# Prompt attention of a hybrid encoder step: p in two rounded parts as stationary operand, v's parts and ones moving, and the streams' first k loaded earlier

## What is computed

```python
def fox_block(qi, cq, qpos, k, v, ck):
    logits = jnp.einsum('bqhd,bkhd->bhqk', qi, k, preferred_element_type=jnp.float32) * scale
    logits = logits + cq[..., :, None] - ck[..., None, :]
    mask = jnp.arange(k.shape[1])[None, :] <= qpos[:, None]
    logits = jnp.where(mask, logits, -jnp.inf)
    p = jax.nn.softmax(logits, axis=-1).astype(v.dtype)
    return jnp.einsum('bhqk,bkhd->bqhd', p, v)
```

## Time and profile before

| | us |
|---|---|
| median of 3 runs | 4081.55 (4078.66 to 4081.91) |
| the profiled execution's own time | 4079.91 |
| its span | 4078.4 |
| the stretch with the prompt's attention | 785 to 1785 of the span |
| TensorE busy in it | 945.66 of 1000 |
| VectorE and ScalarE busy in it | 495.96 and 370.97 |

### The profile page before, as it was taken

How to read it: one execution, slowest core, us unless ns; L and a number is a source line. 1 busy time by engine, 2 the same in 40 slices (tenths; PEclk the granted TensorE clock), 3 DMA queues, 4 the chain that set the end, 5 groups by cost and what they waited for, 6 DMA issues and landing times. The chain is left out here.

```text
span 4078.4 us, 55142 instructions
## 1 busy us (share of the span) xinstructions
PE 3826.5 (94%) x20813; PEld 3215.9 (79%) x20813; DVE 1643.1 (40%) x3406; ACT 1237.3 (30%) x2275; POOL 379.5 (9%) x367
## 2 busy tenths in 40 slices
PE   7999999699999999999979979999999999799996
PEld 7999999577777777776744449999999999677875
DVE  4000476555545455444323324444444444332122
ACT  4111222233333343332113333333333333222122
POOL 3000000211111111121100000000000000021122
PEclk9999999799999999999889989999999999899998
DMA  4221221411122111134233221111111111441221
GB/s 146 68 67 63 66 67 64 88 37 46 35 45 57 43 38 36 40 116 146 102 107 105 93 74 45 45 42 45 51 49 42 45 45 35 135 131 49 85 85 56
DMA packets 319131, 278.63 MB, mean 68 GB/s; under 512 B 121314, under 2 KB 269394, under 8 KB 318887
## 3 DMA queue, kind: packets, MB, share of 16 engines
q1 hardware_dynamic: 298703, 247.21, 20.5%
q0 software_dynamic: 5040, 18.09, 1.3%
q10 hardware_dynamic: 15228, 11.10, 1.0%
HBM read 190.70 MB, written 85.65 MB: 68 GB/s over the span
## 5 line engine op out<-in xcount | busy, mean ns | idle before, releaser
L2337 PE MATMUL bank<-hn_hi,up_w_parts 128*128 128x436 f32 (+1 forms) x3520 | 981.5, 360 | 10.1 <-DVE up_w_parts L2412 10.1
L2337 PEld LDWEIGHTS bank<-hn_hi,up_w_parts 128*128 128x128 f32 x3520 | 661.9, 188 | 42.0 <-issue 10.2
L2337 PE MATMUL bank<-hn_lo,up_w_parts 128*128 128x436 f32 (+1 forms) x1760 | 632.7, 359 | 0.0
L2337 PEld LDWEIGHTS bank<-hn_lo,up_w_parts 128*128 128x128 f32 x1760 | 331.3, 188 | 19.2
L332 PE MATMUL bank<-proj_wh,proj_xh 128*128 128x256 f32 (+1 forms) x1088 | 309.6, 285 | 0.0
L332 PE MATMUL bank<-proj_wh,proj_xl 128*128 128x256 f32 (+1 forms) x1088 | 306.7, 282 | 0.0
L332 PE MATMUL bank<-proj_wl,proj_xh 128*128 128x256 f32 (+1 forms) x1088 | 306.7, 282 | 0.0
L2383 ACT COPY up_raw<-bank 128x436 f32<-128x436 f32 (+1 forms) x220 | 110.5, 502 | 641.9 <-PE bank L2337 611.9
L1432 PE MATMUL bank<-heads_p_pT,heads_p_v 128*65 128x512 f32 (+3 forms) x640 | 288.2, 532 | 10.3 <-issue 10.1
L2586 PE MATMUL bank<-down_w_hi,down_g_hi 128*128 (+1 forms) x748 | 237.7, 400 | 50.1 <-DVE down_g_lo L2681 42.7
L2681 DVE TENSOR_TENSOR down_g_lo<-down_g_raw,down_g_hi 128x256 fp32r<-128x256 f32 (+1 forms) x198 | 110.1, 556 | 391.3 <-ACT down_g_hi L2646 391.3
(11 more groups left out here) (404 smaller groups left out, 6634.9 us busy)
## 6 DMA issues: line engine op xcount, KB each, us to landing
up_w<-in_w_up_dram SPq DMA_DIRECT2D x44, 512.0 KB, 4.7
down_g_raw<-scratch_g SPq DMA_DIRECT2D x88, 256.0 KB, 2.6
scratch_g<-up_acc SPq DMA_DIRECT2D x88, 218.0 KB, 2.0
heads_s_k<-in_cache_fox_k_dram SPq DMA_DIRECT2D x8, 2048.0 KB, 12.6
heads_s_v<-in_cache_fox_v_dram SPq DMA_DIRECT2D x8, 2048.0 KB, 8.1
heads_d_qkvT<-scratch_gch SPq DMA_DIRECT2D x17, 768.0 KB
down_y<-in_w_down_dram SPq DMA_DIRECT2D x22, 512.0 KB, 3.7
scratch_gch<-proj_work SPq DMA_DIRECT2D x48, 218.0 KB, 1.9
```

The lines of the kernel that those rows point to most:

```text
L2337: mm = pe.matmul(bank[:, pair(n) + e, 0:width], w_parts[:, a, part, e, k, :], x[:, k, cols], start=(k == 0 and m == 0), stop=(k == KD - 1 ...
```

## The change

p is now kept in two float32r parts. ScalarE takes exp twice for each block, once rounded into `p_hi` and once in float32 into `p`; VectorE subtracts them into `p_lo`. v is split once per head into `v_parts`, 130 columns a block: v's high part (64), two columns of ones, v's low part (64). The product is turned round: for each 128 queries of a block, `p_hi` (128 x 128) is stationary and all 130 columns of `v_parts` move, then `p_lo` is stationary and the first 66 columns move. The fourth tile of 128 queries has no room for 130 columns in the bank, so its `p_hi` goes in two products, of 66 and of 64 columns. The result stands as queries by columns, so the four transposes of each group go; ScalarE copies 128 x 456 (`raw`), and VectorE adds the parts and divides. v has one buffer for loading in place of two; f, its sums and the rows of c lie in places of p. k and q of the two parities are tensors of their own, and the streams' k of streams 0 and 1 is laid in those of even heads and loaded in the prompt's last head. The planned times are set anew.

```diff
-    PERIOD = 72.0
+    PERIOD = 66.0
...
-    SPEED = 0.62
+    SPEED = 0.57
...
-            return 2.65e-3 * sum(self.width(G, b) for b in range(self.blocks(G))) + 0.95e-3 * first + 1.6 + \
+            return 2.0e-3 * sum(self.width(G, b) for b in range(self.blocks(G))) + 0.95e-3 * first + 1.2 + \
...
-            pe.wait_ge(s["p_ready"], u + 1)
-            pe.matmul(self.bank[0:self.FD + 1, self.out, BANK - wide:BANK], self.v[:, h % 2, b, :],
-                      self.pT[:, u % 3, BANK - wide:BANK], start=(b == 0), stop=(b == last)).then_inc(s["pv_mm"], 1)
+            pe.wait_ge(s["lo_ready"], u + 1)
+            for i in range(4 - wide // P, 4):
+                cols, out = slice(i * P, (i + 1) * P), self.bank[:, self.out, i * VW:i * VW + (VW if i < 3 else VS)]
+                hi, lo = self.p_hi[:, u % 3, cols], self.p_lo[:, u % 2, cols]
+                last = b == 4 * g + 3
+                pe.matmul(out, hi, v[:, 0:VW if i < 3 else VS], start=(b == 0 and i == 0), stop=False)
+                if i == 3:
+                    pe.matmul(out[:, 0:FD], hi, v[:, VS:VW], start=False, stop=False)
+                mm = pe.matmul(out[:, 0:VS], lo, v[:, 0:VS], start=False, stop=last)
+            mm.then_inc(s["pv_mm"], 1)
...
-            nc.scalar.activation(self.pT[:, u % 3, BANK - wide:BANK], self.bank[:, self.keys[u % 2], BANK - wide:BANK],
-                                 ACT.Exp).then_inc(s["p_ready"], 1)
+            nc.scalar.activation(self.p_hi[:, u % 3, cols], logits, ACT.Exp)
+            after(act, s["lo_ready"], u - 1)
+            nc.scalar.activation(self.p[:, u % 2, cols], logits, ACT.Exp).then_inc(s["p_ready"], 1)
...
-            if G >= 1:
-                act.wait_ge(s["row_mm"], self.use["o", G - 1] + 1)
-            nc.scalar.copy(self.oT[:], self.bank[0:self.FD + 1, self.out, :]).then_inc(s["oT_ready"], 1)
+            after(act, s["o_ready"], 2 * G)
+            nc.scalar.copy(self.raw[:], self.bank[:, self.out, 0:self.RAW]).then_inc(s["raw_ready"], 1)
...
+            nc.scalar.copy(self.v_parts[:, h % 2, :, 0:FD], self.v[:]).then_inc(s["v_hi"], 1)
...
+            dve.wait_ge(s["p_ready"], u + 1)
+            after(dve, s["pv_mm"], u - 1)
+            nc.vector.tensor_tensor(self.p_lo[:, u % 2, cols], self.p[:, u % 2, cols],
+                                    self.p_hi[:, u % 3, cols].bitcast(F32), ALU.subtract).then_inc(s["lo_ready"], 1)
...
+            nc.vector.tensor_tensor(self.v_parts[:, h % 2, :, self.VS:self.VW], self.v[:],
+                                    self.v_parts[:, h % 2, :, 0:FD].bitcast(F32), ALU.subtract).then_inc(s["v_lo"], 1)
...
+            nc.vector.reciprocal(self.inv[:, a, 0:3], three[:, :, FD]).then_inc(s["inv_ready"], 1)
+            nc.vector.reciprocal(self.inv[:, a, 3:4], fourth[:, FD:FD + 1]).then_inc(s["inv_ready"], 1)
+            tt(three[:, :, 0:FD], three[:, :, 0:FD], three[:, :, VS:VW], ALU.add).then_inc(s["inv_ready"], 1)
...
-        yield self.prompt.end - 30.0
+        last_head = (self.prompt.FH - 1) * self.prompt.NG
+        yield self.prompt.group_at[last_head + 2]
+        sp.wait_ge(self.prompt.s["pv_mm"], self.prompt.first_key[last_head + 1])
         load_k(0)
+        load_k(1)
```

More of the change, by code:

```diff
@@ L1340, in sums @@
             pe.wait_ge(s["f_step"], NB)
-            pe.matmul(out, c["tri"][:], self.f[:].rearrange("p n h -> p (n h)"), start=True, stop=False)
-            pe.matmul(out, c["ones"][:], self.before[:].rearrange("p n h -> p (n h)"), start=False, stop=True) \
+            pe.matmul(out, c["tri"][:], self.f.rearrange("p n h -> p (n h)"), start=True, stop=False)
+            pe.matmul(out, c["ones"][:], self.before.rearrange("p n h -> p (n h)"), start=False, stop=True) \
                 .then_inc(s["row_mm"], 1)
@@ L1415, in keys_tensor @@
             after(pe, s["p_ready"], u - 1)
[L1416 to L1417 removed]
+            pe.matmul(out, self.k_hi[a][:, keys], self.q_both[a][:, cols], start=True, stop=False)
+            mm = pe.matmul(out, self.k_lo[a][:, keys], self.q_hi[a][:, cols], start=False, stop=b < 4 * g)
             if b >= 4 * g:
@@ L1470, in keys_scalar @@
             u, wide = self.first_key[G] + b, self.width(G, b)
+            logits, cols = self.bank[:, self.keys[u % 2], BANK - wide:BANK], slice(BANK - wide, BANK)
             yield at + 1.6
@@ L1736, in tensor @@
                 pe.wait_ge(self.prompt.s["row_free"], len(self.prompt.uses))
+                pe.wait_ge(self.prompt.s["raw_ready"], self.prompt.groups)
             turn_k(0, n)
@@ L1876, in vector @@
         yield self.begin + 0.3
-        dve.wait_ge(self.prompt.s["row_free"], len(self.prompt.uses))
+        dve.wait_ge(self.prompt.s["o_ready"], 2 * self.prompt.groups)
         nc.vector.memset(self.q_heads[:], 0.0).then_inc(s["new_ready"], 1)
```

168 lines of the change are left out of this document (94 added, 74 removed).

## The result

The changed kernel takes **4174.33 us** (median of 4 runs, 4168.61 to 4183.89), the kernel before 4080.2 (4 runs, 4078.66 to 4081.91): a ratio of 1.0234 (1.0218 to 1.025). It is slower by 94 us where 46 were forecast. The direction was right and the time lies in the range, near its upper end, but the added time is twice the predicted one.

The account below looks back on a forecast made before the run. TensorE was taken to bound the prompt's stretch; +46 (product with v) - 15 (transposes) + 15 (waits) + 0 (rest) on 4079.9 gave 4126 us, 1.1% slower. Range 4090 to 4180 with 0.70, 4083 to 4185 for 8 in 10.

Parts of the forecast that it names:

- The bound: In the prompt's attention, 785 to 1785 us, TensorE sets the pace: busy 946 us of 1000, VectorE 496, ScalarE 371.
- The load of p's parts: Product with v on TensorE: 2,496 products at 0.112 us each, 280 us against 234, so 46 us longer.
- Rival A: Product with v: loads hide or are quicker than read; 3955 us, or 4048 at 0.081 us a product; chance 7%.
- The transposes: TensorE's 128 transposes of finished groups go, 9 us, with the 6.6 us waited before them: -15 us.
- The waits: TensorE's waits, mostly on VectorE, grow with its busy share: +15 us, between -20 and +60.
- VectorE and ScalarE: In the prompt's stretch ScalarE goes from 371 to about 549 us, VectorE from 496 to about 722; both stay beside TensorE.
- Rival C: VectorE or ScalarE takes over at L1513's wait on the second exp: 0.3 us a block, 96 us, 4207 us; chance 7%.
- The clock: TensorE in the prompt's stretch was expected to stay at full clock, with no time added for it in the sum.
- Rival D: Narrow products lower TensorE's clock: a tenth of the prompt's 1,045 us at 1.2 GHz adds about 50 us, 4176; chance 4%.
- The planned times: Order on the engines: the product stands 4.0 planned units behind its logits as before; the new times were costed at nothing.
- The early k: The streams' first two k loads move into the prompt's last head: nothing gained, bounds -5 and +5 us.
- Rival B: Added time falls where TensorE stood idle, 40 of 54 us closing: 4086 us; 10% for within 0.2%, 2% for faster.

Follow-up runs that it names:

- the best version here: The changed kernel with v's parts stationary, p's parts moving, and the high products ahead of the wait for p's low part: 4069.35 us, ratio 0.9971.

## Why the prediction was right in direction and wrong in size

- **The bound was read rightly.** TensorE sets the pace in the prompt's stretch, before and after.
- **The load of p's parts: right.** Forecast were loads 0.11 us apart and 2,496 x 0.112 = 280 us; the timeline shows 0.112, and the account 274, 0.110 each. The product of before holds 239 us, not 234. The term is +35 for a forecast of +46. Rival A, that the loads hide, is out. The Trainium skill, "TensorE: Matmul & The Clock Gate", section "Back-to-back issue gap", has 0.081 us for such pairs, and the timeline's 0.112 speaks against it here. The choice was made by the row with 4 moving columns, the right one.
- **What a narrow product does to the one behind it: left out.** The first wide product behind one of 66 columns ends 0.07 to 0.08 us later than behind a wide one (0.31 against 0.24): +13 us in all. The prediction said that a load hides only behind a product that is longer, and applied this to the new products but not to their successor.
- **The transposes: right.** -16 for -15.
- **The waits: the sum was nearly right, by luck; the working wasn't.** Of idle time, 6.6 us went with the transposes, and +15 was forecast on top; TensorE's idle time went from 55 to 66.5, so +18 on top. But the forecast grew all waits on VectorE with its busy share. What grew is one wait, that on p_lo before L1436, by 27 us, while those of `Delta`, of the maxima and of the turning of q and k shrank by 11. The text had called this chain covered, "since the product stands in TensorE's list as far behind its logits as before (4.0 planned units), with more work between". With an exp and a subtraction more in the chain, the same distance did not cover it. The mark that was set, over 60 us of idle time that ends with L1563 or L1513, is not reached: 26.6 and 3.6.
- **VectorE and ScalarE: as forecast, a little less.** 698 and 510 us of the 1,100 for 722 and 549. Rival C has fallen as a sum: its place, the wait of L1513 for the second exp, holds 81 us, 0.25 us for each of 320 blocks where it had 0.3, but little of it reaches TensorE. The row maxima queued behind end 3.6 us of L1375's idle time, and p's low part itself 26.6 of L1436's, where the rival had 96.
- **The clock: the step that failed.** The sum took the prompt's stretch at full clock, and so the clock at nothing. Full clock was named as a mark, and is what is not there. Another mark, TensorE busy for 25 to 40 us longer, shows the same: it is busy for 86 us longer (1031.5 for 945.9), and for 31 when the clock's 55 are taken off. Rival D had the mechanism (narrow moving parts in runs of nine), the price (about 50 us) and the time (4176, measured 4174.3), but a chance of 4%. The account shows +55. Without it the two profiles are 49 us apart, for a forecast of 46: the small misses above cancel, which is luck. What led to 4% was the 1.00 of the stretch before, which holds for a stream of wide products; the only row with few moving columns, 2015 to 2020, stood at 0.50 and was put aside as too far. The trace of before shows more there than was read: in 2010 to 2015, ahead of that row, TensorE is busy 5.00 of 5.00 us, mostly with the same products of 16 moving columns (L859), and the clock falls in it (0.84), so it had fallen once behind narrow products without any idle time. Two thirds of the new products move 66 columns or fewer, so the new stretch lies between the two rows, and the chance should have been far above 4%.
- **How the clock and the wait hang together** was not seen at all: taking the wait away gives back 27 us as idle time and 24 to 34 by the clock. A wait of TensorE was priced at its own length, while in this stretch of narrow products these cost about twice that; where all products are 256 wide, the same waits (38.4 us) bring no more than 3.4 us at 1.2 GHz.
- **The planned times: costed at nothing, worth 47 us** in this kernel, and 10 to 28 where the clock doesn't fall. The prediction looked at the distance of 4.0 units, which both orders have. Since what was built had the better times, this error did not enter the sum.
- **The early k: right**, nothing (1.0234 against 1.0238). Rival B is out as well: in `Delta` and around it 11 us of idle time closed, but in all TensorE's grew by 12.

## What to carry to other kernels

Make the wide operand the one that moves. Two rounded parts of p save TensorE 31 to 43 us of work if they move (208 and 196 against 239), and cost 35 if they are loaded, before the clock has its share. Even so the best version here is only 0.3% faster than plain float32, since the waits take most of what is saved. When a change makes most products narrow, look at the clock as a term of the sum with a price per wait, not as a remote rival; and let the products that need only the first part of an operand go ahead of the wait for the second.

## What the runs showed of the hardware that was not expected

- TensorE's clock falls to 1.2 GHz in a stream of products with 130, 66 and 64 moving columns and stays there for up to 27.3 us though the profile shows no gap of the engine (26.00 busy of 26.00). The same stream with 256 columns, with the same waits, keeps 2.4 GHz (3.4 against 116.1 us at 1.2), and is faster for it. Which property of the narrow products does it, isn't shown.
- More to move can cost less than it saves: 256 columns in place of 64, 66 or 130 cost 45 us of work, and gave back 56 by the clock and 16 at the logits that follow.
- A float32r product of 256 columns behind a load of its own ends 0.12 us after the one before it here (ends at 1400.17, 1400.30, 1400.41 and 1400.54), as in the stage `project` (0.118). The account's 0.128 (2,496 of them in 320 us) is more, since it holds what the first product of a block takes after other work or a wait:

```profile
1399.89 0.28 PE L1441 MATMUL bank<-heads_p_v_parts,heads_p_p_lo 128*128 128x256 f32 x1
1400.02 0.28 PE L1438 MATMUL bank<-heads_p_v_parts,heads_p_p_hi 128*128 128x256 f32 x1
1400.13 0.28 PE L1440 MATMUL bank<-heads_p_v_parts,heads_p_p_hi 128*128 128x256 f32 x1
1400.26 0.28 PE L1441 MATMUL bank<-heads_p_v_parts,heads_p_p_lo 128*128 128x256 f32 x1
```

- The executions of after differ by 15 us, and the longer ones have the lower clock (0.962 to 0.966). Those of before differ by 3 in the same measurement, and by up to 9 beside the later runs (4076.82 to 4085.79), again mostly with the clock (0.971 at 4085.26, 0.974 at 4077.04): time that is lost to the clock varies from one execution to the next.
